# A two-layer hybrid backbone on one core: modulation in two passes, a tile's affine moved into the expert blocks, and another order of the experts

## The reference

```python
x = layer_norm(ALPHA * x + gate * out, ln_g, ln_b)       # post_norm after the mixer
h = x * (1 + scale) + shift                              # mod_in, per token kind
g_sel = argmax(h @ w_rg + b_rg)                          # one of 4 groups
top_v, top_i = top_k(e_logits_in_that_group, 2)          # two of its 8 experts
hb = silu(xb @ w_gate[e]) * (xb @ w_up[e])               # expert e: 1024 -> 512 -> 1024
y += (hb @ w_down[e]) * gate_weight
x = layer_norm(ALPHA * x + gate2 * y, ln_g2, ln_b2)
```

## Time and profile before

| | |
|---|---|
| time, median of 3 runs | 1408.15 us (1406.35 to 1408.94) |
| the profiled execution | 1406.97 us, its span 1405.2 us |
| PE busy | 1056.9 us (75%) |
| DVE busy | 432.2 us (31%) |
| POOL busy | 255.9 us (18%) |
| ACT busy | 160.3 us (11%) |
| chain that ended last | DMA 38%, PE 34%, DVE 11%, issue 10% |
| read from HBM | 379.66 MB, 283 GB/s over the span |
| granted PE clock, mean | 0.872 |

### The profile page before, as it was taken

The page is one execution under the profiler, slowest core; times in us unless marked ns, Lnnn a source line. Parts: engine busy times, 40 slices in busy tenths (PEclk is TensorE's granted clock), DMA queues, the critical chain, the costliest instruction groups (busy, mean ns, idle before and its releaser), DMA issues.

```text
span 1405.2 us, 26607 instructions
## 1 busy us (share of the span) xinstructions
PE 1056.9 (75%) x9716; PEld 536.0 (38%) x9717; DVE 432.2 (31%) x1118; ACT 160.3 (11%) x412; POOL 255.9 (18%) x450
## 2 busy tenths in 40 slices
PE   4899998697688786666556999878837567788680
PEld 1334345444344443323223444444434223344350
DVE  0120217778412121101035001585871101122117
ACT  0110026400000000000012000552000000000000
POOL 2000001301133332212112010000022212333230
PEclk9999997998599999757677999899959868999896
DMA  9867892107989999999965992201079999999922
GB/s 369 291 250 269 312 361 108 57 19 255 416 329 404 415 415 414 415 416 416 414 262 135 131 160 101 75 1 61 30 301 412 415 414 416 415 377 414 414 107 110
DMA packets 85414, 389.75 MB, mean 277 GB/s; under 512 B 17612, under 2 KB 18124, under 8 KB 57720
## 3 DMA queue, kind: packets, MB, share of 16 engines
q1 hardware_dynamic: 63136, 349.77, 63.1%
q0 software_dynamic: 15200, 36.74, 9.6%
q10 hardware_dynamic: 7032, 2.68, 0.7%
HBM read 379.66 MB, written 17.44 MB: 283 GB/s over the span
## 4 chain that ended last, share of the span: by engine, by line
DMA 38%; PE 34%; DVE 11%; issue 10%; ACT 3%; DVEq 2%; POOLq 1%; SPq 1%; POOL 0%; ACTq 0%; PEldq 0%
DMA ring<-in_w_up_dram 21%; PE ps L820 15%; DMA ring<-in_w_down_dram 13%; PE ps L1071 7%; PE ps L1086 4%; PE ps L972 3%; DMA ring<-in_w_ada_dram 2%; PE ps L796 1%; DVEq L1108 1%; POOLq L458 1%; DMA qkv<-ybuf 1%; PE ps L917 1%; PE ps L905 1%; PE ps L939 1%; DVE ps L1272 1%
## 5 line engine op out<-in xcount | busy, mean ns | idle before, releaser
L1071 PE MATMUL ps<-ring,xs 128*32 128x256 f32 x4928 | 330.5, 424 | 109.6 <-DMA ring<-in_w_up_dram 89.1
L1071 PEld LDWEIGHTS ps<-ring,xs 128*32 128x32 f32 x4928 | 177.5, 120 | 250.6 <-issue 166.8
L820 PE MATMUL ps<-ring,hT 128*128 128x512 f32 x576 | 257.0, 606 | 8.1 <-ACT hT L649 4.3
L1086 PE MATMUL ps<-ring,hm 128*32 128x256 f32 x2464 | 167.3, 415 | 87.4 <-DVE hm L1552 79.8
L820 PEld LDWEIGHTS ps<-ring,hT 128*128 128x128 f32 x576 | 110.4, 194 | 153.8 <-issue 143.4
L1086 PEld LDWEIGHTS ps<-ring,hm 128*32 128x32 f32 x2464 | 75.9, 116 | 178.4 <-DVE hm L1552 119.6
L1551 DVE TENSOR_TENSOR hp<-sg,ps 128x128 f32<-128x128 f32 x73 | 21.0, 287 | 388.0 <-ACT sg L756 384.1
L548 POOL DMA_INDIRECT xg<-xmod,idx x77 | 80.9, 1051 | 66.0 <-issue 38.7
L756 ACT ACTIVATE sg<-ps 128x128 f32<-128x128 f32 x73 | 20.3, 278 | 622.9 <-PE ps L1071 622.9
L561 POOL DMA_INDIRECT ybuf<-yo,idy x73 | 75.3, 1031 | 64.4 <-POOL idy L558 64.4
L972 PE MATMUL ps<-ring,qT 128*128 128x512 f32 x192 | 84.7, 601 | 2.0 <-DVE qT L1362 1.6
(11 more groups left out here) (269 smaller groups left out, 790.9 us busy)
## 6 DMA issues: line engine op xcount, KB each, us to landing
ring<-in_w_gate_dram SPq DMA_DIRECT2D x82, 1024.0 KB
ring<-in_w_up_dram SPq DMA_DIRECT2D x82, 1024.0 KB
ring<-in_w_down_dram SPq DMA_DIRECT2D x82, 1024.0 KB
ring<-in_w_ada_dram SPq DMA_DIRECT2D x48, 1024.0 KB, 8.1
ring<-in_w_qkv_a_dram SPq DMA_DIRECT2D x12, 1024.0 KB, 5.1
ring<-in_w_qkv_b_dram SPq DMA_DIRECT2D x12, 1024.0 KB, 16.9
modb<-mdram POOLq DMA_DIRECT2D x12, 512.0 KB, 6.9
qkv<-ybuf SPq DMA_DIRECT2D x6, 1024.0 KB, 8.3
```

The source lines that it names most:

```text
L820: ins = mm(ps[:, 2 * t + hf, :], lhs[:, k, t * P:(t + 1) * P], raw[:, slot, kk * D + hf * 512:kk * D + (hf + 1) * 512], start=(k == 0), st ...
L1071: ins = mm(ps[j * BLK:(j + 1) * BLK, 1, 0:W].rearrange("p (a f n) -> p a f n", a=2, f=G), xs[:, k, :], w[:, :, kk * DE:(kk + 1) * DE].rear ...
L1086: ins = mm(ps[j * BLK:(j + 1) * BLK, 5, 0:WD], hm[:, 2 * c + q, :], ring[:, slot + GU + c, q * D + j * WD:q * D + (j + 1) * WD], start=(c ...
```

## The change

The normalised row is not written any more before the modulation: `(x - mean) * modb`, then `* rstd + modb'`, written to `o` in its own column order. Tiles 0 and 1 get their affine in two passes of the same form, from the unnormalised row. Tile 2's are two DVE passes behind the output copies of expert blocks 0 and 1, with the affine rows now loaded into `modb` as well; the second affine is loaded by POOL behind the third block. `wr` is loaded in natural order, one transfer per matrix; PE's turns of `o` and the transpose of the experts' input read with a stride of 8 columns instead. The key of an expert is its index times (352 less its pairs), scaled by 32 and with the index added, so that equal products keep the order of the indices; it needs the counts in a row, three more matmuls, and comes later.

```diff
@@ gpsimd
-                load_affine(l, 0)
+                load_affine(l, 0, lnb)
 ...
-                last = x[:, NT - 1, :]
-                chain(pool.tensor_tensor(last, last, lnb[:, 2, :], ALU.mult))
-                pool.tensor_tensor(last, last, lnb[:, 3, :], ALU.add).then_inc(x2_done, 1)
                 pool.wait_ge(mod_used, l + 1)
                 load_gates(l, 1)
-                if l == 1:
-                    load_affine(l, 1)
+                load_affine(l, 0, modb)
 ...
                 for lane in range(LANES):
                     body(lane, lane, (2, 0, 1)[lane])
+                pool.wait_ge(x2_done, l + 1)
+                load_affine(l, 1, modb)
 ...
-                if l == 0:
-                    load_affine(l, 1)
@@ scalar
-                    rows = w[l].rearrange("(j r h b) n -> b r j h n", j=G, h=2, b=G)
-                    for b in range(G):
-                        for j in range(G):
-                            load_wr(wr[b * BLK:(b + 1) * BLK, l, 2 * j:2 * j + 2, lo:hi], rows[b, :, j])
+                    load_wr(wr[:, l, :, lo:hi], w[l].rearrange("(p k) n -> p k n", k=KD))
@@ tensor
-                        transpose_tiles(lambda t: o[:, t, :], xm_rdy[l], xT_ps[l], by_run, (t,))
+                        transpose_tiles(lambda t: o[:, t, :], xm_rdy[l], xT_ps[l], by_stride, (t,))
 ...
-                    ins = mm(ps[0:NE, 5, 0:1], a_all[:, t, :], ones[:, 0:1], start=(t == 0), stop=(t == NT - 1))
+                    mm(ps[0:NE, 5, 0:1], a_all[:, t, :], ones[:, 0:1], start=(t == 0), stop=(t == NT - 1))
+                for t in range(NT):
+                    ins = mm(ps[0:1, 5, 64:64 + NE], ones[:, 0:1], a_all[:, t, :], start=(t == 0), stop=(t == NT - 1))
                 ins.then_inc(rt_pe[l], 1)
+                running(0)
+                running(1)
                 pe.wait_ge(key_rdy, l + 1)
 ...
+                running(2)
@@ vector, layer_norm_rows
-                    rsqrt(rstd[:, 0:1], var[:, 0:1], newt[:, 0:1], newt[:, 4:5])
-                    chain(v.tensor_scalar(x[:, t, :], x[:, t, :], mv[:, t, 0:1], rstd[:, 0:1], ALU.subtract, ALU.mult))
-                    chain(v.tensor_tensor(t1[:, :], x[:, t, :], modb[:, sc, :], ALU.mult))
-                    v.tensor_tensor(o[:, t, :].rearrange("p (j b r) -> p j r b", j=G, b=KD),
-                                    t1[:, :].rearrange("p (j r b) -> p j r b", j=G, b=KD),
-                                    modb[:, sc + 1, :].rearrange("p (j r b) -> p j r b", j=G, b=KD),
-                                    ALU.add).then_inc(xm_rdy[l], 1)
+                    r = rstd[:, 4 + t:5 + t]
+                    rsqrt(r, var[:, 0:1], newt[:, 0:1], newt[:, 4:5])
+                    chain(v.scalar_tensor_tensor(t1[:, :], x[:, t, :], mv[:, t, 0:1], modb[:, sc, :], ALU.subtract, ALU.mult))
+                    v.scalar_tensor_tensor(o[:, t, :], t1[:, :], r, modb[:, sc + 1, :], ALU.mult, ALU.add)\
+                        .then_inc(xm_rdy[l], 1)
                     dve.drain()
                     if t < NT - 1:
-                        scale_rows(t, lnb)
+                        chain(centre_rows(t, lnb))
+                        chain(spread_rows(t, lnb))
+            def centre_rows(t, rows):
+                return v.scalar_tensor_tensor(x[:, t, :], x[:, t, :], mv[:, t, 0:1], rows[:, 2, :], ALU.subtract, ALU.mult)
+            def spread_rows(t, rows):
+                return v.scalar_tensor_tensor(x[:, t, :], x[:, t, :], rstd[:, 4 + t:5 + t], rows[:, 3, :], ALU.mult, ALU.add)
@@ vector, routing
-                v.tensor_scalar(one_row(1400, NE), iota[0:1, 0:NE], picked[:, 0:1], -200.0, ALU.is_equal, ALU.mult)
-                chain(v.tensor_scalar(seen, iota[0:1, 0:NE], picked[:, 1:2], -100.0, ALU.is_equal, ALU.mult))
+                v.tensor_scalar(one_row(1400, NE), iota[0:1, 0:NE], picked[:, 0:1], -2.0 * LEAD, ALU.is_equal, ALU.mult)
+                chain(v.tensor_scalar(seen, iota[0:1, 0:NE], picked[:, 1:2], -LEAD, ALU.is_equal, ALU.mult))
                 chain(v.tensor_tensor(one_row(1400, NE), one_row(1400, NE), seen, ALU.add))
-                v.tensor_tensor(one_row(1400, NE), one_row(1400, NE), iota[0:1, 0:NE], ALU.add).then_inc(key_rdy, 1)
 ...
                 dve.wait_ge(rt_pe[l], 2)
+                chain(v.tensor_scalar(seen, ps[0:1, 5, 64:64 + NE], -1.0 * NE, 352.0 * NE + 1.0, ALU.mult, ALU.add))
+                chain(v.tensor_tensor(seen, seen, iota[0:1, 0:NE], ALU.mult))
+                v.tensor_tensor(one_row(1400, NE), one_row(1400, NE), seen, ALU.add).then_inc(key_rdy, 1)
 ...
-                dve.wait_ge(x2_done, l + 1)
@@ vector, experts
-                    v.transpose(xs[:, :, :].rearrange("p k n -> p (k n)"), xg[:, lane, :]).then_inc(xs_rdy[l], 1)
+                    v.transpose(xs[:, :, :], xg[:, lane, :].rearrange("p (r b) -> p b r", b=KD)).then_inc(xs_rdy[l], 1)
 ...
                     body(lane, lane, LANES, 0)
+                    if lane == 0:
+                        dve.wait_ge(lnb_ld, 160 * l + 128)
+                        chain(centre_rows(NT - 1, modb))
+                    if lane == 1:
+                        spread_rows(NT - 1, modb).then_inc(x2_done, 1)
+                        dve.drain()
```

More of the change, by code:

```diff
@@ L58 @@
 BIG = 1e30
+LEAD = float(2 ** 19)
 F32 = mybir.dt.float32
@@ L448, in load_gates, with load_affine @@
                     pool.dma_start(dst[:, cnd, :], rows(l, cnd, 3 * stage + 2)).then_inc(lnb_ld, 16)
-            def load_affine(l, stage):
-                dst = modb if stage else lnb
+            def load_affine(l, stage, dst):
                 for i, w in enumerate((ln_g, ln_b)):
@@ L986, in turn_x @@
                         for k in range(4 * h, 4 * h + 4):
-                            ins = nc.tensor.transpose(tile_ps(t)[:, k * P:(k + 1) * P], by_run(o[:, t, :], k), ident)
+                            ins = nc.tensor.transpose(tile_ps(t)[:, k * P:(k + 1) * P], by_stride(o[:, t, :], k), ident)
                         ins.then_inc(xT_ps[l], 1)
@@ L1005, in _ @@
                 if l == 0:
-                    pe.wait_ge(ld_wr, 16 * LAYERS * (2 * G * G + 2))
+                    pe.wait_ge(ld_wr, 16 * LAYERS * 4)
                 turn_x(1)
@@ L1023, in _, with running @@
                 for t in range(NT):
-                    ins = mm(ps[0:NE, 5, 0:1], a_all[:, t, :], ones[:, 0:1], start=(t == 0), stop=(t == NT - 1))
+                    mm(ps[0:NE, 5, 0:1], a_all[:, t, :], ones[:, 0:1], start=(t == 0), stop=(t == NT - 1))
+                for t in range(NT):
+                    ins = mm(ps[0:1, 5, 64:64 + NE], ones[:, 0:1], a_all[:, t, :], start=(t == 0), stop=(t == NT - 1))
                 ins.then_inc(rt_pe[l], 1)
+                def running(t):
+                    for i in range(t + 1):
+                        mm(ps[:, 7, t * NE:(t + 1) * NE], tri if i == t else ones, a_all[:, i, :],
+                           start=(i == 0), stop=(i == t))
+                running(0)
+                running(1)
                 pe.wait_ge(key_rdy, l + 1)
@@ L1157, in fold @@
             def fold(l, stage):
-                dve.wait_ge(lnb_ld, 64 * (2 * l + stage + 1))
+                dve.wait_ge(lnb_ld, 160 * l + 64)
                 dve.wait_ge(mod_ld, 64 * (l + 1))
@@ L1167, in layer_norm_rows @@
             def layer_norm_rows(l):
-                dve.wait_ge(lnb_ld, 64 * (2 * l + 1))
+                dve.wait_ge(lnb_ld, 160 * l + 64)
                 for t in range(NT):
@@ L1210, in take_experts @@
                 if t == 0:
-                    dve.wait_ge(lnb_ld, 64 * (2 * l + 1) + 32)
+                    dve.wait_ge(lnb_ld, 160 * l + 96)
                 chain(v.tensor_tensor(t1[:, :], ysum[:, t, :], modb[:, 0 if t == 0 else 1, :], ALU.mult))
@@ L1410, in _ @@
                 dve.wait_ge(lg_rdy, l + 1)
-                dve.wait_ge(ld_wr, 16 * LAYERS * (2 * G * G + 2))
+                dve.wait_ge(ld_wr, 16 * LAYERS * 4)
                 chain(v.tensor_tensor(lg[:, 0], ps[:, 7, 0:36], br[:, l, :], ALU.add))
@@ L1595, in _ @@
                     dve.wait_ge(hT_ps[1], NT)
-                    dve.wait_ge(lnb_ld, 64 * 2)
+                    dve.wait_ge(lnb_ld, 160)
                     for k in range(KD // 2, KD):
@@ L1602, in _ @@
                 else:
-                    dve.wait_ge(lnb_ld, 64 * 4)
+                    dve.wait_ge(lnb_ld, 320)
                     finish(0)
```

## The result

Over the runs of both kernels on one chip, the changed kernel takes 1393.72 us in the median (1389.78 to 1395.17, 4 runs) and the kernel before 1407.25 us (1405.80 to 1408.94, 4 runs): ratio 0.9899, 95% interval 0.9875 to 0.9923. It is faster by 13.5 us where 25.5 were forecast, and inside the range. The profiled execution took 1394.03 us, its span is 1392.2 us.

A forecast was written before the change was run, and what follows sets the result against it. The bound was taken to change hands between DVE, PE and DMA, with layer 1 ending on PE. Savings of 4.7 (layer 0's start) + 2.9 (its end) + 17.9 (layer 1) = 25.5 us gave 1382.7 us, range 1373 to 1397.

The forecast's parts named there:

- the late copy in layer 0: POOL's 1 MB affine load among layer 0's expert blocks: falls into idle DMA, gathers unaffected, cost 0.
- Layer 0's routing: Before layer 0's experts: shorter tile 2 passes and no wait for POOL start the expert stage 4.7 us earlier.
- The late copy leaves layer 0's end: End of layer 0: without that copy there, the first expert outputs land faster, saving 2.9 us.
- Layer 1's routing: Before layer 1's experts: picks ready 3.7 + 4.0 = 7.7 us earlier, so first weights go out earlier.
- POOL's part: Layer 1's routing: two one-row DVE instructions no longer wait for POOL's affine passes, saving 4.0 us.
- the 2.3 us for tile 2's start: Layer 1's routing: PE's last projection starts 1.4 us earlier, and DVE starts tile 2 2.3 us earlier.
- Layer 1's experts: Layer 1's expert stage: 10.2 us of the layer's 17.9, with 12.0 from the order and a copy costing 3.1.
- The stalls: Layer 1's weight loads: full buffers hold DMA 4 us behind expert 30's run and 0.5 at expert 14, 4.5 together.
- The mark that I had set for this: Layer 1's weight stream: SP's queue pausing over 10 us behind expert 30 would show the prediction wrong.
- (a): Rival, layer 1: the order buys nothing, as early heavy experts idle DMA 12 us more; 1394.7 us, chance 0.15.
- (b): Rival, routing of both layers: POOL's copies keep DVE's little instructions locked out; 1390.2 us, chance 0.11.
- (c): Rival, expert blocks: strided transpose outgrows its cover in PE-bound blocks; 1423 us if it takes 3.0 us, chance 0.04.

The follow-up runs named there:

- act_copy_five_b: Changed kernel with the late affine copy issued from ACT's queue, behind the fifth block's SiLU in layer 0 and the third's in layer 1: 1382.82 us.
- copy_end: Changed kernel with the late affine copy moved behind the last expert block in both layers: 1386.02 us.
- before_no_pool: Kernel before, without POOL's two passes over the last tile and the wait for them; values change: ratio 1.0036, total not read.
- pool_back: Changed kernel with POOL's two passes put back before its copies, DVE's passes kept; values change: ratio 1.0206, total not read.
- act_copy_idle_b: Changed kernel with the late copy issued by ACT behind the sixth block in layer 0 and the twenty-fourth in layer 1: 1382.12 us.
- the second profile of the changed kernel: Profile from running the unaltered changed kernel once more, beside two others on the same chip: median 1391.11 us.
- act_copy: Changed kernel with the late affine copy issued from ACT's queue behind the third block's SiLU in both layers: 1383.96 us.
- before_order: Kernel before with only the new order of the experts (changed key and its three matmuls, running sums ahead of it): 1395.93 us.

## Why the prediction was right or wrong, step by step

**The step that failed** is the late copy in layer 0: "gathers, two blocks ahead; the issues cost 1.1 us of POOL: 0". I counted what the two instructions cost POOL (they do take 1.2 us) and what the megabyte costs the DMA engines, and left out what it does to the queue that it stands in. And "two blocks ahead" is ahead of the matmuls: DVE transposes the rows a block earlier. The one issued at 399.27 was wanted at 405.3 (411.52 less the 6.21 that DVE waited), 6.0 us later, and 6.0 us is what a gather takes in the median. In act_copy_five_b the same block's gather has 6.85 us (issued at 396.22, transposed from 403.07), so the two issues had taken 0.8 of the room: they were not free either. There was no room left, and behind the copy it took 12.12. PE lost 5.1 us, and the next block ran partly at the lower clock (granted clock 0.60 from 412.0 to 418.3; 5.89 us against 3.64 for the 64 matmuls). The fifth weight load, which sets the pace of the rest of the stage, moved with it: it went out at 423.46, which is 50.2 us behind the first block instead of 43.2. What is measured is +7.0 and +6.4 where I had 0. The copy may fall into slack of the weights' stream, as argued; the gather behind it has none. In layer 1 the copy delays a gather as well (11.2 us) and PE waits 4.2 us for it, but behind it PE still waits for weights: the stage is no shorter with the copy in ACT's queue (324.2 and 323.1 us against 323.5 and 321.3).

**Layer 0's routing** (4.7): -6.2 and -5.0 to the first matmul, -6.3 and -6.0 to the first gather's issue. The logits are read 14.77 us behind tile 2's start in the first profile and not 19.81: 5.0, for 4.9 worked out; in the second it is 13.99, so 5.8. What goes beyond the forecast differs between the two and comes with PE's clock, which the sum did not have (last section).

**The late copy leaves layer 0's end** (2.9): 39.7 to 36.9 and 36.8, and back to 39.6 in copy_end. Confirmed.

**Layer 1's routing** (7.7): -6.6 in each execution. POOL's part is right (4.0; before_no_pool shows 4.0, pool_back 4.1) and tile 2's own 1.4 as well. What is missing are 1.2 of the 2.3 us for tile 2's start (1.1 measured: 43.51 to 42.39 us behind the first projection). The timeline of the changed kernel, beside the earlier trace rows:

```profile
967.60 27.73 PE L964 MATMUL ps<-ring,qT 128*128 128x512 f32 x64 [0.39 <-DVE qT L1331]
996.05 13.90 PE L964 MATMUL ps<-ring,qT 128*128 128x512 f32 x32
1009.99 1.22 DVE L1175 TENSOR_TENSOR t<-ps,kT 128x1024 f32<-128x1024 f32 x1 [1.59 <-PE ps L964]
1025.43 0.37 SPq L386 DMA_DIRECT2D ring<-in_w_gate_dram  x1
```

"PE's last projection starts 1.4 us earlier": it doesn't. PE's first two projections run 27.73 us without a gap, in both kernels, and the last starts 28.45 us behind the first (28.44 before: 965.21 to 993.65). Tile 0's rows had been ready before PE was. So PE sets tile 2's start, and DVE, which was to be the bound, waits 1.59 us.

**Layer 1's experts** (17.9 less 7.7: 10.2): -8.9 and -11.0. The order brought 11.8 by itself for 12.0. The copy cost 1.0 to 3.2 by copy_end and 2.9 to 4.0 by act_copy_idle_b, for 3.1. The stalls are where they were put. SP's last issue before the pause behind expert 30 and the first after it, and the DMA share before them:

```profile
1226.85 3.62 SPq L386 DMA_DIRECT2D ring<-in_w_down_dram  x2
1248.21 0.36 SPq L386 DMA_DIRECT2D ring<-in_w_gate_dram  x1
```

```profile
1130.00:1150.00 20.00, 16.67 (x306) 9.32 (x298) 4.80 (x12) 0.83 (x3) 7.46 (x13) 1.00 0.92 361
1150.00:1235.00 85.00, 67.24 (x1168) 37.25 (x1164) 19.16 (x48) 3.33 (x12) 29.58 (x49) 0.98 1.02 415
```

Idle are 20 x 0.08 = 1.6 us behind expert 21 and 4.1 behind 30, 5.7 for 4.5 worked out. The mark that I had set for this was bad: SP pauses 17.7 us (1230.5 to 1248.2), well over the 10 that were to show the prediction wrong, yet the engines still have about 15 us of transfers queued when the pause begins (15.3 from issue to landing in the prediction); the time is lost only beyond that.

**Sum.** Of 25.5 the second profile of the changed kernel shows 18.3 (0.2 + 5.0 - 6.4 + 2.8 - 0.7 + 6.6 + 11.0 - 0.2), and the gather is most of the difference, 6.4 of 7.2. That run is the fastest of its six; by the medians the change brings 13.5 and 15.7 us, and 10 to 12 are missing. Without the stall the forecast's figure is met: act_copy and act_copy_five_b come out at 1384.0 and 1382.8 for 1382.7. Part of this agreement is luck, as smaller misses cancel: in the profile of act_copy layer 0's routing brings 7.6 us for 4.7, layer 1's routing 6.6 for 7.7 and its experts 8.1 for 10.2. Two of the marks set beforehand failed, both by the stall: layer 1's first weights go out at 1025.4 and 1022.2, not near 1014, and PE does wait for the strided transpose once in layer 0's run of blocks, though the transpose only waits for its gather.

**The rivals.** (a) "The order buys nothing" is out: before_order. (b) "POOL's copies lock DVE out" is out: 0.22 to 0.23 us with the copies issued beside them. (c) "The transpose outgrows its cover" is out: 642 ns, and the blocks behind the stall are 6.5 us apart. The changed kernel's time (1393.7, 1391.1) is near those of (a) and (b), 1394.7 and 1390.2, by a cause that was none of the three. The range held because it had been drawn wide enough for those two.

Open: the time to layer 0's output projection (281.8 to 284.5), layer 1's attention (210.4 to 213.3) and layer 0's routing (86.9 to 90.1 with the changed kernel's code) differ between executions; what makes the first two differ was not looked into.

## What to carry to other kernels

The late copy had three costs here: its issue, its share of the DMA engines, and its place in a queue. Before a large copy is moved into slack, look at which small, latency-bound transfers follow it in the same engine's queue, and issue it from another engine if they are needed soon; here this brought 8 to 10 us on top of the change's 14 to 16. When a step is said to start earlier because its input is ready earlier, check that the engine that does it is free then.

## What the hardware showed that was not expected

PE's running sums between the tables (small matmuls, 128x32) took 2.77 us in the kernel before, where PE had waited 4.18 us for DVE:

```profile
352.39 0.48 PE L1024 MATMUL ps<-cst,kT 128*32 128x1 f32 x6 [4.18 <-DVE kT L1437]
353.48 2.77 PE L1032 MATMUL ps<-kT,cst 128*128 128x32 f32 x12
```

```profile
353.00:356.00 3.00, 2.82 (x16) 2.80 (x16) 1.37 (x10) 0.21 (x1) 0.00 (x0) 0.50 1.03 434
```

and in the changed one, where it had waited 0.78:

```profile
351.06 0.35 PE L1016 MATMUL ps<-cst,kT 128*32 128x1 f32 x6 [0.78 <-DVE kT L1443]
```

```profile
351.00:354.00 3.00, 2.81 (x36) 2.25 (x36) 2.25 (x16) 0.21 (x1) 0.00 (x0) 1.00 1.03 429
```

The second fence of each is the busy time by stretch. The granted clock is 0.50 in the first stretch (1.2 GHz) and 1.00 in the second (2.4 GHz), and twelve of these matmuls take 2 x 0.85 us for 2.77. The wait in front of them goes with it in all thirteen profiles of layer 0: after 0.7 to 1.5 us of waiting six of them take 0.86 us at most, after 4.0 to 5.2 us 1.38 at least (in pool_back 1.49 after 5.24).

It is not a gain of the change, though. The second profile of the changed kernel has the slow sums again, because PE's work in front of them had run at the full clock and was done early:

```profile
337.05 1.98 PE L989 MATMUL ps<-wr,qT 128*128 128x36 f32 x16 [0.24 <-ACT qT L732]
346.63 0.35 PE L1016 MATMUL ps<-cst,kT 128*32 128x1 f32 x6 [4.03 <-DVE kT L1443]
347.10 1.49 PE L1023 MATMUL ps<-kT,cst 128*128 128x32 f32 x6
```

The router's logits take 1.98 us there against 3.62 in the first profile, and the adaLN product behind them 3.64 against 5.64. The granted clock was 1.00 from 339 to 342.6 us, and 0.50 from 342 to 345 in the first profile. So each execution of the same code has its slow stretch at another place of layer 0's routing, and gains some of what the forecast did not have: 6.3 and 6.0 us to the first gather for 4.7. In front of the slow stretch of the first profile PE had waited 3.12 us for DVE (`turn_x(2)`, L979), at the same place in the second 1.50; what made these waits differ was not looked into.

A pass of GpSimd over 128x1024 (2.36 us) holds up a VectorE instruction on one row of 4 or 32 numbers, for nearly its whole length when that comes early in it. The Trainium skill, SBUF — State Buffer (Who interferes with whom), says that the two share a pair of ports, and that whoever comes second is blocked, not slowed. The trace agrees on the blocking, with 1.95 to 2.55 us against 0.22. On the order it does not show this clearly: in pool_back the blocked instruction is stamped at 335.77 and POOL's pass at 335.91, and it still ends with that pass.
